# A hybrid decoder layer on one Trainium2 core: the second half of the tokens takes all experts of the retrieval layer in dense matmul steps

## The reference

```python
v1, i1 = lax.top_k(s1, PEER_TOPK)
v2, i2 = lax.top_k(s2, PEER_TOPK)
...
top_score, pos = lax.top_k(cand_score, PEER_TOPK)
expert_id = jnp.take_along_axis(cand_id, pos, axis=-1)
gate = jax.nn.softmax(top_score, axis=-1)
...
u_sel = u_tab[idb].astype(jnp.float32)
act = jax.nn.gelu(jnp.einsum('tkd,td->tk', u_sel, xb.astype(jnp.float32)), approximate=False)
return jnp.einsum('tk,tkd->td', gb * act, v_tab[idb].astype(jnp.float32))
```

## Time and profile before

| | us |
|---|---|
| runs of the kernel | 1740.11, 1725.96 |
| their median | 1733.03 |
| span of the profiled execution (first to last instruction) | 1657.0 |
| what lies around the span, by the two runs | 69.0 to 83.1, by the median 76.0 |

### The profile page before, as it was taken

How to read it: one execution, slowest core, us unless ns; L and a number is a source line. 1 busy time by engine, 2 the same in 40 slices (tenths; PEclk the granted TensorE clock), 3 DMA queues, 4 the chain that set the end, 5 groups by cost and what they waited for, 6 DMA issues and landing times.

```text
span 1657.0 us, 16021 instructions
## 1 busy us (share of the span) xinstructions
PE 1355.5 (82%) x5078; PEld 669.4 (40%) x5078; DVE 1063.8 (64%) x2871; ACT 348.9 (21%) x776; POOL 775.5 (47%) x848
## 2 busy tenths in 40 slices
PE   8999899888788978877769876678877778788777
PEld 7866574432455644642213320122332333333323
DVE  4625249957777889976555766444565666666656
ACT  2321422211342322011002120021122222222221
POOL 3000005766676657775467777355433333334332
PEclk9999999999998989997779997689999998998999
DMA  4223807999999999999999999999999999999995
GB/s 154 77 102 115 299 25 269 380 411 412 409 409 409 411 396 409 408 409 411 398 411 409 409 410 411 418 412 417 420 422 422 421 421 422 422 421 422 421 422 224
DMA packets 130212, 599.35 MB, mean 362 GB/s; under 512 B 15824, under 2 KB 15824, under 8 KB 97360
## 3 DMA queue, kind: packets, MB, share of 16 engines
q0 software_dynamic: 115776, 536.92, 80.3%
q1 hardware_dynamic: 14208, 61.15, 9.6%
q10 hardware_dynamic: 144, 0.26, 0.0%
HBM read 596.18 MB, written 2.10 MB: 361 GB/s over the span
## 4 chain that ended last, share of the span: by engine, by line
DMA 44%; PE 27%; DVE 12%; POOL 8%; issue 6%; ACT 2%; DVEq 1%; ACTq 0%; SPq 0%; POOLq 0%
DMA arena<-in_peer_uv,arena 21%; DMA arena<-in_peer_v,arena 14%; DMA arena<-in_peer_u,arena 9%; PE psum L1152 7%; DVE arena L1906 5%; POOL arena L752 4%; POOL arena L740 4%; PE psum L1130 4%; PE psum L1083 3%; PE psum L816 3%; PE psum L827 3%; PE psum L1064 2%; DVE arena L1537 1%; ACT arena L1428 1%; PE psum L838 1%
## 5 line engine op out<-in xcount | busy, mean ns | idle before, releaser
L1906 DVE CUSTOM_DVE_ANT_0 arena<-arena,psum 128x1024 f32<-128x1024 f32 x512 | 622.9, 1218 | 417.7 <-DMA arena<-in_peer_uv,arena 245.8
L1152 PE MATMUL psum<-arena 128*128 128x512 f32 x880 | 426.5, 642 | 98.3 <-ACT arena L1428 98.3
L740 POOL DMA_INDIRECT arena<-in_peer_u,arena x288 | 272.4, 946 | 363.4 <-PE psum L893 226.0
L1130 PE MATMUL psum<-arena 128*32 128x512 f32 x1152 | 278.5, 726 | 128.6 <-DMA arena<-in_peer_v,arena 128.5
L772 POOL DMA_INDIRECT arena<-in_peer_uv,arena x220 | 207.1, 941 | 335.2 <-PE psum L1152 299.1
L752 POOL DMA_INDIRECT arena<-in_peer_v,arena x288 | 271.5, 943 | 147.1 <-issue 76.8
L1152 PEld LDWEIGHTS psum<-arena 128*128 128x128 f32 x880 | 176.1, 205 | 352.6 <-issue 217.7
L1130 PEld LDWEIGHTS psum<-arena 128*32 128x32 f32 x1152 | 47.3, 120 | 313.9 <-DMA arena<-in_peer_v,arena 224.1
L816 PE MATMUL psum<-arena 128*128 128x512 f32 x256 | 118.5, 609 | 2.5 <-DVE st L1579 2.4
L1083 PE MATMUL psum<-arena 128*128 128x512 f32 x224 | 98.7, 593 | 1.4 <-ACT arena L1355 1.4
L827 PE MATMUL psum<-arena 128*128 128x256 f32 x384 | 93.0, 402 | 8.3 <-ACT arena L1211 7.0
(11 more groups left out here) (271 smaller groups left out, 1395.0 us busy)
## 6 DMA issues: line engine op xcount, KB each, us to landing
arena<-in_w_in SPq DMA_DIRECT2D x28, 1024.0 KB, 7.8
arena<-in_w_out SPq DMA_DIRECT2D x16, 512.0 KB, 7.9
arena<-in_peer_w_q SPq DMA_DIRECT2D x16, 512.0 KB, 14.0
arena<-in_peer_w_q SPq DMA_DIRECT2D x8, 1024.0 KB, 13.2
arena<-in_peer_u,arena POOLq DMA_INDIRECT x292, 15.5
arena<-in_peer_v,arena POOLq DMA_INDIRECT x292, 15.9
arena<-in_peer_uv,arena POOLq DMA_INDIRECT x220, 27.3
arena<-in_x SPq DMA_DIRECT2D x4, 512.0 KB, 5.1
```

The source lines that it names most:

```text
L740: pool.indirect_dma_start(row, None, u_d, bass.IndirectOffsetOnAxis(ap=eid[i % 2][:, c:c + 1], axis=0)).then_inc(landed, 16)
L1130: mm = pe.matmul(bank[6 + half][group * UK:(group + 1) * UK], zrows[k % 2][:, z0:z0 + ZW], row[:, half * 512:(half + 1) * 512], start=Fals ...
L1152: mm = pe.matmul(bank[y_bank[i][half]], diag_w[q % 2][:, j], row[:, D + half * 512:D + (half + 1) * 512], start=False, stop=c == SEL - 1 o ...
L1906: dve.tensor_tensor_reduce(row, row, h2p[i], 1.0, 0.0, ALU.mult, ALU.add, dots[:, c:c + 1]).then_inc(s["u_free"], 1)
```

## The change

Tiles 0 and 1 (n = 0 to 255) gather as before, and all their rows go by `gather_u` and `gather_v`; the pair gathers and their table are gone. Tiles 2 and 3 gather nothing. In their place each engine walks a second list, DENSE, after its n loop: 64 steps of two second-key values each. Step i loads 1 MB of a transposed u table and 1 MB of the v table by plain DMAs on SP's queue. "u" multiplies the u block with the inputs of both tiles (2 keys x 8 chunks, 16 matmuls with 256 moving columns); ACT takes the Gelu of 128x512; DVE multiplies it by the gate matrix G; "v" multiplies the result with the v block (2 keys x 2 tiles x 2 halves, 8 matmuls with 512 moving columns) and adds into four PSUM banks.

G is a dense matrix of gates: for 256 tokens and 128 first keys by 64 second keys per pass, so there are two passes (0 and 1). For each token DVE builds two one-hot matrices over its 128 selections ("pick" with the gates, and "place"), and PE multiplies them (128x64). A batch ("g") is 8 tokens, in two sub-batches of 4 tokens, for which there are two buffers. Pass 0 (32 batches) is at n = 267 to 282 in the loop; pass 1 is put in the dense list, two batches behind each "u" from step 4 of the list on.

The choice of experts for tiles 2 and 3 has 11 links instead of 13 and goes to other places: up to three links behind each product from n = 230 on, and as many as 11 at once after n = 255.

```diff
+def dense_choices(at):
...
+                if n <= place["s", t, h // 2]:
+                    n, room = place["s", t, h // 2] + 1, 0
+                if room == (3 if n < GATHERED else DENSE_LINKS):
+                    n, room = n + 1, 0
+                LINK_AT.setdefault(n, []).append((t, h, link))
...
+    later = [("g", 1, b) for b in range(BATCHES)]
+    out = [("yd", t, half) for t in DENSE_T for half in range(2)] + [("u", 0, 0), ("u", 0, 1)]
+    for n in range(STEPS):
+        out.append(("v", 0, n))
+        if n + 2 < STEPS:
+            out.append(("u", 0, n + 2))
+        if n >= 4:
+            out += later[2 * (n - 4):2 * (n - 3)]
...
 # SP
+                else:
+                    sp.wait_ge(*filled("u", 0, n - 2))
+                sp.dma_start(u_slot[slot], peer_ut[n]).then_inc(ut_in[slot], 16)
...
+                else:
+                    sp.wait_ge(s["v_done"], n - 1)
+                sp.dma_start(v_slots[slot], v_step_d[n].rearrange("i (j d) -> i j d", j=STEP_KEYS)).then_inc(vt_in[slot], 16)
...
 # PE
+                    for q in range(BATCH // SUB):
+                        m = (t * BATCHES + i) * (BATCH // SUB) + q
+                        pe.wait_ge(s["ab_rdy"], m + 1)
...
+                elif kind == "u":
...
+                    for k in range(STEP_KEYS):
+                        for c in range(DC):
+                            mm = pe.matmul(ps[:, 2 * P * k:2 * P * (k + 1)].rearrange("p (t c) -> p t c", t=2), u_slot[slot][:, k, c],
+                                           h2T_both[:, :, c * P:(c + 1) * P], start=c == 0, stop=c == DC - 1)
...
+                elif kind == "v":
+                    slot, turn_ = v_slot(i)
+                    pe.wait_ge(s["w_rdy"], i + 1)
+                    pe.wait_ge(vt_in[slot], 16 * turn_)
...
 # DVE
+                        for j in range(SUB):
+                            dve.tensor_scalar(pick[m % 2][:, j], keyno, key[:, 0, n + j:n + j + 1], key[:, 2, n + j:n + j + 1], ALU.is_equal, ALU.mult)
+                        dve.tensor_tensor(place_[m % 2], keyno[:, t * PASS_KEYS:(t + 1) * PASS_KEYS].unsqueeze(1).to_broadcast([P, SUB, PASS_KEYS]),
+                                          key[:, 1, n:n + SUB].unsqueeze(2).to_broadcast([P, SUB, PASS_KEYS]), ALU.is_equal).then_inc(s["ab_rdy"], 1)
...
+                    dve.wait_ge(*read("u", 0, i))
+                    dve.tensor_tensor(w, w, G[part][:, :, first:first + STEP_KEYS].rearrange("p t k -> p k t"), ALU.mult).then_inc(s["w_rdy"], 1)
```

471 lines of the change are left out of this document (257 added, 214 removed).

## The result

| | before | after |
|---|---|---|
| runs (us) | 1740.11, 1725.96 | 2331.77, 2322.24 |
| median | 1733.03 | 2327.01 |
| span of the profiled execution | 1657.0 | 2330.0 |

The changed kernel is slower: ratio 1.3471, with a 95% interval of 1.3239 to 1.3704. The forecast was 2260 us with a range of 2185 to 2380. The direction and the range held, the time itself was 67 us too low, and that hides more than it shows: the span is 146 us over the forecast span of 2184. Of these 58 lie before the product of n = 255, 43 in pass 0 and 45 in the dense steps; against them stand 76 us that I had put around the span and that are not there.

The account below looks back on a forecast made before the run. The kernel before was taken to be bound by gathered bytes, the dense steps by PE. 1155 (start) + 883 + 118 + 24 + 4 gave a span of 2184 us; with 76 around it, 2260 us, range 2185 to 2380.

Parts of the forecast that it names:

- 76 us that I had put around the span: Outside the profiled span: 76 us (69 to 83 by the two runs), kept unchanged and added to the span of 2184.
- The step that decides: Dense steps: PE needs 13.8 us a step against 5.1 us of transfer, so 64 steps take 883 us.
- a lower clock in the ordinary steps: Rival, dense steps: PE at a mean clock of 0.90, 883 us become about 970, time 2350 us; chance 0.07.
- late loads: Rival, dense steps: a step's loads take 20 us, each "u" waits 6 us, 2640 us in all; chance 0.04.
- the 95 us for three links behind each product: DVE from n = 230 to 255: products, links, norm, weighting and waits take 95 us, ending the last product at 985.
- the 5 us for weighting and waits: DVE from n = 230 to 255: weighting of a unit and waits between chained links, an estimated 5 us.
- 57 us were forecast (7, 3, 1 and 46): DVE behind n = 255: ten links 7, tile 2's gates 3, last weighting 1, six heads of tile 3 46 us.
- 80 for pass 0, 15 + 3, the tail of 12 + 3.4: Before the first "u": pass 0 80, last two heads 15, tile 3's gates 3, PE's tail 12, "yd" matmuls 3.4 us.
- The value of 1.25 us for a sub-batch: Gate matrix: DVE builds one sub-batch in 1.25 us, from four at 0.22, 0.32 and 0.05 for the semaphore.
- its floor of 0.84: Gate matrix: PE's four 128x64 matmuls take 0.84 us, a lower limit for one sub-batch.
- the gain of 30 us: Gate-matrix builders on DVE: if the skill's tensor_scalar rule held in full, some 30 us less; left out of the sum.
- 118 + 24 = 142 us: Pass 1, 16 steps with gates: PE waits 7.4 us each, 118 us, plus 1.5 us each for lower clock, 24.

Follow-up runs that it names:

- no_pass1: Changed kernel with the second pass of the gate matrix left out, the later steps reusing the first pass's gates; 2069.7 us.
- warm0: Changed kernel with one unused matmul of 512 columns added to each sub-batch of pass 0; 2256.3 us.
- g_ahead: Changed kernel with a step's two gate batches ahead of the next "u" instead of behind it, on every engine; 2174.2 us, ratio 1.3125.
- bf16_gates: Like bf16_b, with the one-hot matrices also in bfloat16 and no added matmuls in pass 0; ratio 0.9238 to the kernel before.
- after_again: The changed kernel unedited, run again on one chip beside the kernel before; 2306.38 us, ratio 1.3419.
- bf16_b: Changed kernel with bfloat16 dense steps, more buffers, pass 1 spread over 30 steps ahead of "u", added pass 0 matmuls; ratio 0.9539 to the kernel before.

## Why the prediction was right, and where it was wrong

**The bound.** The step that decides, 64 x 13.8 = 883 us of matmuls, measured 884.9 in no_pass1, at a clock of 1.00 in the 573 us behind the last gates. That PE and not the bytes sets these steps holds: with a quarter of the matmuls they fell from 1074.0 to 561.2 us, and with matmuls four times as fast to 407.2. The rivals of a lower clock in the ordinary steps and of late loads both fell: no wait for a load, DMA share 0.39.

**The 76 us around the span: wrong.** The step "Around the span lie 76 us, which I keep" took a difference between two chips for a constant of the launch. The profiled runs of the changed kernels have 1.7 to 1.9 us there. What the slower chip really adds is in the gathers (n = 255 at 1042.7 instead of 972.5), so that two errors met: with 76 us I carried about the right amount in the wrong place, and the total came out only 67 low. That is luck, and the range held by it: without the 76 us it would have been 2109 to 2304, and 2327 lies above that. On a chip like that of the profile the changed kernel's span would be some 1185 + 1074 = 2259 (warm0, with its equal stages, had 2254.6) against my 2184: 75 us, 3.4%, too low.

**The start, term by term.** The product of n = 255 came at 972.5 on the profile's kind of chip, not 985: the 95 us for three links behind each product were 12 too many. The mechanism was right, since DVE did not wait for a u row between n = 230 and 255 in g_ahead. Too high were the links, 48 us there (0.63 each, not 0.69) where 54 were forecast, and the 5 us for weighting and waits, of which almost nothing came. From there to the first gate matmul 57 us were forecast (7, 3, 1 and 46) and 57.9 came.

**Pass 0: mis-sized.** From the first gate matmul to the first "u" the sum had 113 us (80 for pass 0, 15 + 3, the tail of 12 + 3.4), the trace 155. The value of 1.25 us for a sub-batch was taken for DVE, with PE's 0.84 as a floor under it. DVE needs 1.36 (rows of after: four tensor_scalars begin every 1.36 us when nothing holds them):

```profile
1518.99 1.12 DVE L1868 TENSOR_SCALAR arena<-tri_gt,arena 128x128 f32<-128x128 f32 x4
1520.02 0.43 DVE L1869 TENSOR_TENSOR arena<-tri_gt,arena 128x256 f32<-128x256 f32 x1
1520.35 1.12 DVE L1868 TENSOR_SCALAR arena<-tri_gt,arena 128x128 f32<-128x128 f32 x4
```

which is 7 us more over 64. The larger part, 31 us, goes with PE (155 against 124 in bf16_gates, where PE waits for DVE): its floor of 0.84 was read at full clock and was 1.8 in pass 0. In the sum the clock stood only under pass 1. Some 4 of the 42 us are left without a cause.

Two of the Trainium skill's rules were weighed. The Trainium skill's "TensorE: Matmul & The Clock Gate", Part 1, makes idleness the cause of a low clock. The trace agrees for the fall, since PE was busy 17 of 57 us ahead of pass 0 and the clock there was 0.65. It disagrees for what follows: PE was busy 121 of 135 us in pass 0 at a clock of 0.54; what differs in warm0, at 0.93, is the added 512-column matmuls. The Trainium skill's "VectorE: DVE Perf Modes", the perf-mode tier table, would have made the tensor_scalars half as costly per element as a tensor_tensor. The trace does not show it at this size: four of 128 columns take 1.03 us to the next instruction (1518.99 to 1520.02), 2.0 ns a column, the tensor_tensor of 256 columns 0.33, 1.3 ns. So leaving the gain of 30 us out was right.

**Pass 1: mis-sized.** The mechanism was right: 16 gaps that end on line 1869, the product of the same "u" ahead of the builders. Forecast were 118 + 24 = 142 us, measured 189. To the first sub-batch PE waited 3.2 us (2.8 by my terms: the product takes 1.04 us and not 0.69; it reads G with a stride, which may be why, but no run took the stride away). Then four sub-batches took 6.6 and 7.1 us in the two steps shown where 3 x 1.25 + 0.84 = 4.6 were forecast, PE at 1.2 GHz again, and what is left of the mean of 11.8, some 1.8, is the "v" behind them, against 1.5. By kind, of the 189 us some 55 are PE's waits, 54 the gate matmuls at full speed, and the other 80 I put down to the lower clock (0.81 in that stretch), for which the sum had 24.

What the runs leave open: why some chips gather more slowly. In 345 to 850 us the packets of 4 KB have about the same median time on both (159 ns in after and after_again, 161 in before and g_ahead) and a longer tail on the slower chips (99th percentile 506 to 535 ns against 189 to 192), and TensorE's clock is lower there. Which of these is cause and which effect was not tried.

## What to carry to other kernels

Halving the bytes of a bandwidth-bound kernel is worth only what the engine that pays for it leaves: divide its new work per block by the block's transfer time first (13.8 to 5.1 us here), and try the scheme where that ratio is below one (3.5 to 4.9 us in bfloat16, in the end 11% faster). In a list that several engines share, look for the work that stands directly behind the result it does not need; moving the gates ahead of one "u" and then DVE's builders ahead of one product was worth 84 and 56 us, without an instruction less. And compare a span with the time of its own run before calling the rest overhead: it can be another chip.

## What the runs showed that was not expected

TensorE can be busy nine tenths of the time at half clock. In pass 0, mostly fp32 matmuls of 64 moving columns, it stood at 1.2 GHz for nearly all of 135 us (four in 1.84 us instead of 0.84), and three times the columns cost nothing (155.5 us against 155.0).

The kernel before differs by 4 to 5% between chips (1655 us against 1716 and 1733). In the changed kernel the difference lies in the stretch of the indirect gathers (408 against 358 to 376 GB/s); its dense steps agree to 0.1 us (1074.0 three times).

A plain load that rounds float32 to bfloat16 on its way kept up the full pace: 4.92 us for 2.1 MB read, 426 GB/s, on POOL's queue. The window of bf16_b shows 208 GB/s there, which must be the bytes written, for the page has the same 461.97 MB read from HBM as that of after.
